# A second mixer's gate chain on one Trainium2 core: two channel products placed around the first inverse transform and the turn of z, and a weight panel split inside the boundary before it

## The reference, cut to what matters

```python
proj = h @ mix_w_in                       # 1024 -> 512 (pool) + 3 * 512 (Hyena)
y_pool = pool_mixer(proj[..., :512], ...)  # centred averages, minus self, grouped product
u = short_conv_centred(proj[..., 512:], conv_w, conv_b)   # three taps along the tokens
parts = split(u, 3); z = parts[-1]
for o in range(2):
    z = parts[o] * (irfft(rfft(z, 512) * spec[:, o], 512)[:, :256] + z * bias[o])
x = x + concatenate([y_pool, z]) @ mix_w_out
```

## Time and profile before

| what | us |
|---|---|
| three runs | 1614.51, 1614.99, 1617.83; median 1614.99 |
| the profiled execution's own time | 1618.04 |
| its span, first to last instruction | 1616.2 |
| TensorE busy in it | 1538.8 (95%) |
| VectorE, ScalarE, POOL busy | 1020.1, 761.7, 209.8 |

### The profile page before, as it was taken

How to read it: one execution, slowest core, us unless ns; L and a number is a source line. 1 busy time by engine, 2 the same in 40 slices (tenths; PEclk the granted TensorE clock), 3 DMA queues, 4 the chain that set the end, 5 groups by cost and what they waited for, 6 DMA issues and landing times.

```text
span 1616.2 us, 28137 instructions
## 1 busy us (share of the span) xinstructions
PE 1538.8 (95%) x10380; PEld 1413.2 (87%) x10380; DVE 1020.1 (63%) x1383; ACT 761.7 (47%) x1213; POOL 209.8 (13%) x255
## 2 busy tenths in 40 slices
PE   3989999978999999999999999999999999999997
PEld 3989998977898888999988699999999999899996
DVE  6897777745666546655556765556655569565554
ACT  2444544554545544544444354444544457354443
POOL 1594093310102121000000000000000000000000
PEclk8998999959999999999999999999999999999999
DMA  9886973213655553755533345554555545245551
GB/s 355 298 296 237 313 281 111 91 63 108 211 202 190 198 192 122 302 194 192 176 135 122 117 155 179 181 193 169 182 194 177 177 152 158 79 174 179 193 194 40
DMA packets 80561, 294.30 MB, mean 182 GB/s; under 512 B 9052, under 2 KB 9405, under 8 KB 79917
## 3 DMA queue, kind: packets, MB, share of 16 engines
q1 hardware_dynamic: 75728, 274.97, 48.7%
q0 software_dynamic: 3984, 16.21, 3.1%
q10 hardware_dynamic: 780, 2.18, 0.5%
HBM read 289.13 MB, written 3.15 MB: 181 GB/s over the span
## 4 chain that ended last, share of the span: by engine, by line
PE 83%; DVE 8%; ACT 4%; issue 2%; DMA 1%; POOL 1%; SPq 0%; DVEq 0%; ACTq 0%
PE bank L207 73%; DVE w_lo L191 2%; DVE arena L788 1%; PE bank L1933 1%; PE bank L1214 1%; DMA arena<-ada 1%; ACT arena L303 1%; PE bank L1946 1%; PE bank L2314 1%; PE bank L1110 1%; PE bank L2292 1%; POOL stat L342 1%; PE bank L825 1%; PE bank L410 1%; ACT w_hi L185 1%
## 5 line engine op out<-in xcount | busy, mean ns | idle before, releaser
L207 PE MATMUL bank<-h_hi,w_hi 128*128 128x256 f32 x2344 | 677.6, 289 | 16.9 <-DVE h_lo L1840 7.9
L207 PE MATMUL bank<-h_lo,w_hi 128*128 128x256 f32 x2344 | 668.5, 285 | 0.0
L207 PE MATMUL bank<-h_hi,w_lo 128*128 128x256 f32 x2344 | 668.3, 285 | 0.0
L191 DVE TENSOR_TENSOR w_lo<-raw,w_hi 128x1024 fp32r<-128x1024 f32 x454 | 546.6, 1253 | 115.9 <-ACT w_hi L185 115.2
L185 ACT ACTIVATE w_hi<-raw 128x1024 fp32r<-128x1024 f32 x458 | 457.8, 1049 | 60.9 <-PE bank L207 29.8
L207 PEld LDWEIGHTS bank<-h_hi,w_hi 128*128 128x128 f32 x2344 | 454.4, 194 | 31.9 <-DVE h_lo L1840 8.1
L207 PEld LDWEIGHTS bank<-h_lo,w_hi 128*128 128x128 f32 x2344 | 454.5, 194 | 5.8 <-issue 1.9
L207 PEld LDWEIGHTS bank<-h_hi,w_lo 128*128 128x128 f32 x2344 | 454.2, 194 | 0.0
L632 DVE TENSOR_TENSOR arena<-arena,bank 128x256 f32<-128x256 f32 x132 | 55.4, 420 | 252.1 <-PE bank L207 180.9
L207 PE MATMUL bank<-w_hi,f_hi 128*128 128x512 f32 x528 | 207.6, 393 | 0.3 <-DVE f_lo L637 0.3
L207 PE MATMUL bank<-w_hi,f_lo 128*128 128x512 f32 x528 | 207.2, 392 | 0.0
(11 more groups left out here) (329 smaller groups left out, 1376.1 us busy)
## 6 DMA issues: line engine op xcount, KB each, us to landing
raw<-panels SPq DMA_DIRECT2D x458, 512.0 KB, 4.5
arena<-ada SPq DMA_DIRECT2D x64, 512.0 KB, 5.2
arena<-ada POOLq DMA_DIRECT2D x8, 512.0 KB, 4.0
arena<-rows POOLq DMA_DIRECT2D x4, 512.0 KB, 4.2
spectrum<-arena POOLq DMA_DIRECT2D x2, 1024.0 KB, 7.1
arena<-spectrum POOLq DMA_DIRECT2D x1, 2048.0 KB, 17.8
X<-x_in SPq DMA_DIRECT2D x1, 1024.0 KB, 5.9
arena<-decay ACTq DMA_DIRECT2D x2, 512.0 KB, 5.9
```

Of the source, the lines that this page charges most:

```text
L191: dve.tensor_tensor(w_lo[:, slot, :], raw[:, slot, :], w_hi[:, slot, :].bitcast(F32), ALU.subtract).then_inc(lo_ready, 1)
L207: last = pe.matmul(out_ap, a, b, start=start and n == 0, stop=stop and n == 2)
```

## The change

There are four edits. First, in the boundary, ScalarE splits the fourth panel (M2 + 3) after h_hi of channel 4 and VectorE after h_lo of channel 5; both used to do it first after the boundary. Second, parts 10 and 11 leave the block before inverse(0): part 10 stands between inverse(0) and the turn of z, part 11 between the turn and forward(1). Third, banks: inverse(0) writes banks 6, 7, 0, 1 and no longer 6, 7, 4, 5, so that its wait for all twelve convolutions goes; forward(1) writes 6, 7, 4, 5 and no longer 4 to 7 in order, and waits for the scaling of part 11 before its second half. Fourth, the orders of ScalarE and VectorE follow: VectorE multiplies both halves of the first spectrum before parts 8 to 11, gates before part 10, and does the first half of the second multiply before the splits of M2 + 19 to M2 + 21; ScalarE copies out the grouped product at loop index 7 instead of 9, splits M2 + 18 one index earlier, turns to the second copy of z ahead of the centre tap of part 11, and makes the high parts and the second bias before the splits of M2 + 19 to M2 + 21.

```diff
+        INTO_MIX2 = STAGES.index(("mix2", 0))
...
+                if n == INTO_MIX2 and k == 4:
+                    split_hi(act, FIRST[("mix2", 0)] + 3)
...
+                if n == INTO_MIX2 and k == 5:
+                    split_lo(dve, FIRST[("mix2", 0)] + 3)
...
-        BACK_BANKS = (6, 7, 4, 5)
+        FORWARD_BANKS = ((0, 1, 2, 3), (6, 7, 4, 5))
+        BACK_BANKS = ((6, 7, 0, 1), (6, 7, 4, 5))
...
             for f in range(2):
+                if o and f:
+                    pe.wait_ge(part_scaled, 12)
...
             for c in range(4):
-                if o == 0 and c == 2:
-                    pe.wait_ge(conv_done, 12)
...
-            forward_pe(pe, 0, 0)
-            parts(8, 12)
+            forward_pe(pe, 0)
+            parts(8, 10)
             pe.wait_ge(m2_evac, 4)
             inverse_pe(pe, 0)
+            parts(10, 11)
             turn_z_pe(pe, 1)
-            forward_pe(pe, 4, 1)
+            parts(11, 12)
+            forward_pe(pe, 1)
...
-            act_panels(act, M2 + 3, 4)
+            act_panels(act, M2 + 4, 3)
...
             for j in range(12):
-                split_hi(act, M2 + 7 + j)
+                if j < 11:
+                    split_hi(act, M2 + 7 + j)
+                if j == 10:
+                    split_hi(act, M2 + 18)
+                if j == 11:
+                    evac_z(2)
                 centre(j)
...
-                if j == 9:
+                if j == 7:
                     for g in range(4):
...
-            act_panels(act, M2 + 19, 3)
+            act.wait_ge(panel_used, M2 + 16)
             for b in range(2):
                 act.wait_ge(m2_evac, 2 * b + 2)
                 high(2 * b, 2 * b + 2)
-            evac_z(2)
             bias(1)
+            act_panels(act, M2 + 19, 3)
...
-            dve_panels(dve, M2 + 3, 4)
+            dve_panels(dve, M2 + 4, 3)
...
             for f in range(2):
-                multiply(0, 0, f)
-                for j in (8 + 2 * f, 9 + 2 * f):
-                    scale_part(j)
-                    split_lo(dve, M2 + 7 + j)
-                    taps_of(j)
-            dve.wait_ge(filter_scaled, 2)
-            for c in range(4):
-                gate(0, c)
-            dve_panels(dve, M2 + 19, 3)
+                multiply(0, f)
+            for j in range(8, 12):
+                if j == 10:
+                    dve.wait_ge(filter_scaled, 2)
+                    for c in range(4):
+                        gate(0, c)
+                scale_part(j)
+                split_lo(dve, M2 + 7 + j)
+                taps_of(j)
             low(1, 0, 2)
             low(2, 2, 4)
-            for f in range(2):
-                multiply(1, 4, f)
+            multiply(1, 0)
+            dve_panels(dve, M2 + 19, 3)
+            multiply(1, 1)
             dve_panels(dve, M2 + 22, 4)
```

More of the change, by code:

```diff
@@ L1925, in mix2_loads, with forward_pe @@
                            spectrum.rearrange("o p q c -> p o q c")).then_inc(m2_loaded, 16)
-        def forward_pe(pe, first_bank, o):
+        def forward_pe(pe, o):
             pe.wait_ge(z_evac, MT * (o + 1))
             for f in range(2):
+                if o and f:
+                    pe.wait_ge(part_scaled, 12)
                 for s in range(2):
                     for m in range(MT):
-                        mm = pe.matmul(bank[first_bank + 2 * f + s][:, :],
+                        mm = pe.matmul(bank[FORWARD_BANKS[o][2 * f + s]][:, :],
                                        forward[:, s, m, f * P:(f + 1) * P], z_tok[:, m, :],
@@ L1941, in inverse_pe @@
             for c in range(4):
-                if o == 0 and c == 2:
-                    pe.wait_ge(conv_done, 12)
                 for f in range(2):
                     for s in range(2):
-                        mm = pe.matmul(bank[BACK_BANKS[c]][:, 0:SEQ],
+                        mm = pe.matmul(bank[BACK_BANKS[o][c]][:, 0:SEQ],
                                        product[:, 2 * f + s, c * P:(c + 1) * P], inverse[:, s, f, :],
@@ L2094, in taps_of, with multiply @@
                      conv_done, j + 1)
-            def multiply(o, first_bank, f):
+            def multiply(o, f):
                 k = filters[:, 4 * o + 2 * f:4 * o + 2 * f + 2, :]
@@ L2100, in multiply @@
                     dve.wait_ge(z_spectrum, 4 * o + 2 * f + s + 1)
-                    z = bank[first_bank + 2 * f + s][:, :].unsqueeze(1).to_broadcast([P, 2, 512])
+                    z = bank[FORWARD_BANKS[o][2 * f + s]][:, :].unsqueeze(1).to_broadcast([P, 2, 512])
                     order(dve.tensor_tensor(terms[:, 2 * s:2 * s + 2, :], k, z, ALU.mult))
@@ L2111, in gate @@
                 dve.wait_ge(z_biased, 4 * o + c + 1)
-                order(dve.scalar_tensor_tensor(out=z_sum[:, c % 2, :], in0=bank[BACK_BANKS[c]][:, 0:SEQ],
+                order(dve.scalar_tensor_tensor(out=z_sum[:, c % 2, :], in0=bank[BACK_BANKS[o][c]][:, 0:SEQ],
                                                scalar=filter_scale[:, 4 * o + c:4 * o + c + 1],
```

## The result

The changed kernel took 1608.57 us (median of 16 runs, 1606.10 to 1612.49) against 1616.53 for the kernel before (16 runs, 1614.26 to 1621.23): ratio 0.995, 95% interval [0.994, 0.996], 8.0 us faster. Forecast were 1606.5 us and 8.5 us less than the median then known. The profiled execution has a span of 1606.9 us and its own time is 1608.79.

The account below looks back on a forecast made before the run. TensorE holds 83% of the chain, so only its stops and half-clock stretches can give time. Boundary 4.2 (or 2.6) plus z chain 4.95 taken from 1614.99 gave 1605.9 to 1607.4, forecast 1606.5 us; own range 1604.3 to 1608.7, 8-in-10 range 1603.5 to 1611.0.

Parts of the forecast that it names:

- The boundary: From TensorE's idle time at 833.94 to the row product's end: earlier fourth-panel split gains 4.2 us, or 2.6.
- the half clock: TensorE at granted clock 0.50 (1.2 GHz) from 837.8 to 841.1, behind its idle 2.3 us; 1.6 us of the gain.
- ScalarE's 0.17 us over: ScalarE before h_hi of channel 5: 1.12 us idle takes a 0.95 us split, leaving 0.17 us.
- The z chain: TensorE from part 11's old end to forward(1)'s end: parts 10 and 11 cover the waits, gaining 4.95 us.
- The sum: Whole kernel: 4.2 + 4.95 = 9.1 us gained, or 7.6 where the clock had not fallen.
- A new wait at forward(1): Rival: evac_z(2) or part_scaled 12 comes last at forward(1) and eats the 4.95; 1610.8 to 1612.4 us, chance 0.09.
- the split did not disturb the norm: Rival denied here: the boundary's split delays h_hi 5 and TensorE's token products, no gain there; 1610.0 us, chance 0.06.
- the slower rival: Long wait at forward(1), then TensorE at 1.2 GHz over forward(1) and four token products, 17.8 us more; 1624.3 us, chance 0.03.

Follow-up runs that it names:

- the other set: The changed kernel timed once more beside its two halves, against the kernel before: median 1607.74 us, ratio 0.9934, 10.2 us faster by the medians.

## Why the prediction was right

**The boundary.** Said: 4.2 us with the half clock before, 2.6 without. Measured: 4.20 between the two profiles, 2.66 against the profiles without it. ScalarE's 0.17 us over was 0.19; VectorE's split ended as channel 6's h_lo was due. One margin was a little off: M2 + 4 had 0.7 us in hand and not 1.0.

**The z chain.** Said: 4.95 us. Measured: 4.97 between the two profiles and 5.0 against the others. The margins came as worked out: shifted by 841.35 - 836.99 = 4.36, scale_part(11) was expected at 892.5 and began at 892.31, the copy of z had 1.6 us in hand (done at 890.60) where 1.4 had been said, forward(1) at 892.2 and began at 892.20, inverse(1) at 910.0 and began at 909.96. Putting the parts back one by one brought back the waits that they had been said to cover.

**The sum.** 9.1 us against the profiled execution: its own time fell by 1618.04 - 1608.79 = 9.25. So close a match of two whole executions is partly luck: their starts of the stage, 822.88 and 822.72, happen to lie side by side in a scatter of 4.8 us. Against the median of the three first runs the forecast was 1606.5, 2.1 below the 1608.57 measured. Two things make this up. The median of 16 runs of before is 1616.53, 1.5 above the first three's 1614.99. And I stood between 7.6 and 9.1, where the profiles show the half clock in one execution of four; 1 of 4 gives 7.6 + 0.25 x 1.6 = 8.0, which is the 8.0 measured. That mixture rests on four profiles, and the other set's 10.2 fits it badly, so its match to the tenth is luck. The forecast's own range has a slip: 1607.4 widened by half of 3.3 is 1609.1, not 1608.7; the 1608.57 lies inside both, near the upper end.

**The rivals.** A new wait at forward(1) did not appear, by a margin of 1.6 us, and came when the copy was moved behind it on purpose; the split did not disturb the norm; the slower rival's last step, a clock that stays low over 17.8 us of work, is not what happened behind the 2.19 us stop.

## What to carry to other kernels

Where one engine holds the chain, list its stops in the stage, add up what the same work takes without them, and look for work ready earlier that can stand in each; here two products placed in two gaps gave 2.6 us, and an engine's own idle time between two channels took in a whole split. Work out what comes last next, for each engine in queue order: a delay of 1.4 us, against 0.7 in hand, was enough to make an unmoved instruction the last. When the gain is under 1%, compare stretches of the profile between fixed events, and take more than one profile of before, since a single one may hold a clock level that other executions of the same kernel do not have.

## What the runs showed of the hardware

The fall of the granted clock behind a short stop is not a fixed price. The same 2.37 us stop was followed by 0.50 in one of four profiles; one of 1.62 us, with 0.44 us of idle time shortly ahead of it, and one of 2.19 us were followed by 3.2 us at 0.52 and at 0.56, in the one profile each; behind the stops of 1.24 and 1.23 us the clock did not fall in any of the five profiles that have them. The Trainium skill (TensorE: Matmul & The Clock Gate, Part 1: The HAM clock gate) says that the point where the clock rises varies between runs of one kernel; these profiles show the like of the fall, which came in one and not in the three others. Each time the lower level cost 1.6 to 1.7 us and was over a few us later, with TensorE at work. The other surprise is the start of this stage, which moves by 4.8 us between executions (819.28 to 824.12), though the code ahead of it is the same in those two kernels. All of the scatter of the profiles lies ahead of it: in the 12 that do not move the row product, the rest after forward(1) takes 707.8 to 708.0 us. In the profile of before a window early in the kernel stands at the full level and the like one of the changed kernel at the lower:

```profile
325.90:329.10 3.20, 2.17 (x21) 1.96 (x19) 2.99 (x7) 0.87 (x2) 3.12 (x4) 1.00 0.00 0
```

```profile
326.10:329.30 3.20, 2.78 (x14) 2.41 (x12) 2.99 (x7) 0.98 (x2) 3.12 (x4) 0.50 0.00 0
```

In the next 3.2 us both are at the lower level (0.51 before, 0.50 changed), so the changed kernel's slow stretch there begins about 3 us earlier; from 332.3 to 341.9 both stay at 0.50. Added up in steps of 3 us from 0 to 819, what the lower level takes from a busy TensorE ((1 - granted clock) x busy time) is 31.0 and 29.8 us in the two profiles in which the stage starts first and 36.0 in the one in which it starts last, with 32.0 to 34.7 in the others. So the clock goes the way of the scatter; that it makes up all of it was not shown.
